# The first layer's shift computed with its weights stationary, as columns

## The reference, cut to what matters

```python
def _modulation(cond, w_mod, b_mod):
    m = jax.nn.silu(cond) @ w_mod + b_mod
    return jnp.split(m, 3, axis=-1)
...
sh, sc, g = _modulation(c, w_mod[l], b_mod[l])
shc, scc, gc = _modulation(c_ctx, w_mod[l], b_mod[l])
h = x * (1.0 + sc) + sh
hc = ctx * (1.0 + scc) + shc
q, k, v, z = jnp.split(h @ w_in[l], 4, axis=-1)
...
```

## Time and profile before

| | us |
|---|---|
| median of 3 runs | 1850.63 |
| lowest, highest run | 1850.36, 1851.28 |
| the profiled execution | 1850.39 |
| its span | 1848.6 |
| TensorE busy | 1802.8 (98% of the span) |
| VectorE busy | 1291.5 (70%) |
| ScalarE busy | 928.0 (50%) |
| GpSimd busy | 269.4 (15%) |

### The profile page before, as it was taken

The page is one execution under the profiler, slowest core; times in us unless marked ns, Lnnn a source line. Parts: engine busy times, 40 slices in busy tenths (PEclk is TensorE's granted clock), DMA queues, the critical chain, the costliest instruction groups (busy, mean ns, idle before and its releaser), DMA issues. The chain is left out here.

```text
span 1848.6 us, 30835 instructions
## 1 busy us (share of the span) xinstructions
PE 1802.8 (98%) x10621; PEld 1554.1 (84%) x10621; DVE 1291.5 (70%) x2061; ACT 928.0 (50%) x1680; POOL 269.4 (15%) x219
## 2 busy tenths in 40 slices
PE   7999999999999999989999999999999999999998
PEld 3888888888888888878878889888888888898886
DVE  6677777778687877765868485675848484757658
ACT  2555555555555555560046555464736464554500
POOL 3100000000000000255431010101000010102951
PEclk9999999999999999999999999999999999999999
DMA  9512121312122222225420010101010100101343
GB/s 348 135 47 83 47 82 47 84 38 79 54 74 60 74 60 62 73 94 187 159 80 24 12 45 11 45 0 45 11 45 11 34 23 11 45 11 45 99 143 125
DMA packets 82111, 127.28 MB, mean 69 GB/s; under 512 B 49760, under 2 KB 49920, under 8 KB 81936
## 3 DMA queue, kind: packets, MB, share of 16 engines
q1 hardware_dynamic: 76048, 108.54, 18.7%
q0 software_dynamic: 2384, 8.39, 1.6%
q10 hardware_dynamic: 3632, 9.73, 1.3%
HBM read 108.90 MB, written 20.09 MB: 70 GB/s over the span
## 5 line engine op out<-in xcount | busy, mean ns | idle before, releaser
L548 PE MATMUL acc<-h_hi,w_hi 128*128 128x512 f32 (+1 forms) x1408 | 524.9, 373 | 3.1 <-DVE h_lo L473 1.6
L548 PE MATMUL acc<-h_hi,w_lo 128*128 128x512 f32 (+1 forms) x1408 | 508.7, 361 | 0.0
L548 PE MATMUL acc<-h_lo,w_hi 128*128 128x512 f32 (+1 forms) x1408 | 507.9, 361 | 0.0
L548 PEld LDWEIGHTS acc<-h_hi,w_lo 128*128 128x128 f32 x1408 | 265.3, 188 | 41.5
L548 PEld LDWEIGHTS acc<-h_hi,w_hi 128*128 128x128 f32 x1408 | 265.8, 189 | 40.3 <-DVE h_lo L473 4.7
L548 PEld LDWEIGHTS acc<-h_lo,w_hi 128*128 128x128 f32 x1408 | 266.3, 189 | 33.9
L1676 DVE TENSOR_REDUCE stats<-acc 128x1 f32<-128x1280 f32 x128 | 189.7, 1487 | 43.3 <-PE acc L1775 42.7
L1586 ACT ACTIVATE far_prob<-acc,stats 128x1280 f32<-128x1280 f32 x128 | 170.2, 1330 | 28.3 <-DVE stats L1676 26.5
L1593 ACT ACTIVATE far_pt<-acc 128x512 f32<-128x512 f32 (+1 forms) x192 | 101.1, 527 | 162.0 <-PE acc L1784 158.6
L1775 PE MATMUL acc<-k_dup,q_stack 128*128 128x512 f32 (+1 forms) x768 | 176.7, 367 | 1.8 <-ACT far_prob L1586 0.4
L1797 PE MATMUL acc<-far_pt,far_v 128*128 128x128 f32 x1280 | 172.7, 275 | 0.0
(11 more groups left out here) (208 smaller groups left out, 2906.8 us busy)
## 6 DMA issues: line engine op xcount, KB each, us to landing
w_raw<-in_w_in SPq DMA_DIRECT2D x64, 512.0 KB, 3.3
near_late_slots<-in_w_mod SPq DMA_DIRECT2D x64, 256.0 KB, 2.7
w_raw<-in_w_out SPq DMA_DIRECT2D x16, 512.0 KB, 3.2
w_raw<-y_t POOLq DMA_DIRECT2D x14, 448.0 KB, 5.0
y_t<-y SPq DMA_DIRECT2D x7, 640.0 KB, 3.1
modulation_rows<-in_w_scale SPq DMA_DIRECT2D x8, 512.0 KB, 6.9
modulation_rows<-in_w_mod SPq DMA_DIRECT2D x8, 512.0 KB, 6.7
out_rows<-in_x SPq DMA_DIRECT2D x8, 512.0 KB, 4.5
```

The lines of the kernel that those rows point to most:

```text
L548: mm = nc.tensor.matmul(m.bank(self.bank_of(j, c), w), wt[:, b % 2, k, :], ht[:, k, t0:t0 + w], start=(k == 0 and i == 0), stop=(k == KT - ...
```

## The change

The operands of the shift's products change places. Each piece of weights is now stationary, in eight blocks of 128x128, and the two condition columns move (128x2). Each product is 128x2: both conditions' shift of 128 channels, as columns. The 64 products (8 pieces by 8 blocks) are not added in PSUM; each has its own two columns of bank 3 (`shift_parts`, 128 columns in all). When all are there VectorE adds the eight pieces' with one reduction, then scales by 0.5 and adds the bias with a second operation. `take_rows` on ScalarE and `turn_rows` on TensorE are gone. `cols_done` now goes up to 3. Since only bank 3 is held, TensorE transposes the tokens of n = 0, 1 and 2 ahead of the wait, which stands before n = 3.

```diff
-        self.row_buf = m.k_raw[0:2, 0:D]
+        self.shift_parts = m.psum[:, 3, 0:2 * KT * KT]
...
-    def take_rows(self, act):
-        act.wait_ge(self.piece_used, KT)
-        for half in range(2):
-            self.nc.scalar.activation(self.row_buf[:, half * 512:(half + 1) * 512], self.m.psum[0:2, 2 + half, :], ACT.Copy,
-                                      scale=0.5).then_inc(self.row_ready, 1)
...
-        v.wait_ge(self.turned, 1)
-        first = m.b_cols[:, 0, 0:1]
-        nc.vector.tensor_tensor(m.mod_cols[:, 0, :, 0:KT], m.bank(2, 2 * KT).rearrange("p (k c) -> p c k", c=2),
-                                bass.AP(first.tensor, first.offset, [list(first.ap[0]), [0, 2], [1, KT]]), ALU.add)\
+        v.wait_ge(self.piece_used, KT)
+        shift, first = m.mod_cols[:, 0, :, 0:KT], m.b_cols[:, 0, 0:1]
+        nc.vector.tensor_reduce(shift, self.shift_parts.rearrange("p (k t c) -> p c t k", k=KT, c=2), AX, ALU.add)\
+            .then_inc(self.cols_done, 1)
+        v.wait_ge(self.cols_done, 2)
+        nc.vector.scalar_tensor_tensor(shift, shift, 0.5,
+                                bass.AP(first.tensor, first.offset, [list(first.ap[0]), [0, 2], [1, KT]]), ALU.mult, ALU.add)\
             .then_inc(self.cols_done, 1)
...
-            for half in range(2):
-                mm = nc.tensor.matmul(m.psum[0:2, 2 + half, :], m.cond_act[:, :, k], self.pieces[k][:, half * 512:(half + 1) * 512],
-                                      start=(k == 0), stop=(k == KT - 1))
+            for t in range(KT):
+                mm = nc.tensor.matmul(self.shift_parts[:, 2 * (k * KT + t):2 * (k * KT + t + 1)],
+                                      self.pieces[k][:, t * P:(t + 1) * P], m.cond_act[:, :, k], start=True, stop=True)
             mm.then_inc(self.piece_used, 1)
-
-    def turn_rows(self, pe):
-        pe.wait_ge(self.row_ready, 2)
-        for k in range(KT):
-            mm = self.nc.tensor.transpose(self.m.psum[:, 2, 2 * k:2 * k + 2], self.row_buf[:, k * P:(k + 1) * P], self.m.ident[0:2, 0:2])
-        mm.then_inc(self.turned, 1)
...
-                modulation.take_rows(act)
-                act.wait_ge(modulation.cols_done, 2)
+                act.wait_ge(modulation.cols_done, 3)
...
-                    if n == 2:
-                        modulation.turn_rows(pe)
-                        pe.wait_ge(modulation.cols_done, 2)
+                    if n == 3:
+                        pe.wait_ge(modulation.cols_done, 3)
```

More of the change, by code:

```diff
@@ L208, in __init__ @@
         self.tanh_done, self.cond_ready, self.coef_ready, self.piece_used = sem("tanh"), sem("cond"), sem("coef"), sem("used")
-        self.row_ready, self.turned, self.scale_done, self.cols_done = sem("row"), sem("turned"), sem("scale"), sem("cols")
+        self.scale_done, self.cols_done = sem("scale"), sem("cols")
         self.dve, self.lam_exp = sem("dve"), sem("lam_exp")
-        self.row_buf = m.k_raw[0:2, 0:D]
+        self.shift_parts = m.psum[:, 3, 0:2 * KT * KT]
         self.unused = [b[:, 0:D] for b in (m.gate, m.y)]
```

## The result

| | before | changed |
|---|---|---|
| median, us (12 runs each) | 1850.36 | 1854.64 |
| lowest and highest, us | 1850.04, 1851.30 | 1854.00, 1856.39 |
| profiled execution, us (its span) | 1850.39 (1848.6) | 1854.89 (1853.0) |
| its mean granted clock of TensorE | 0.999 | 0.991 |

The changed kernel takes 1.0024 times the time of before, 95% interval 1.0016 to 1.0031: slower by 4.28 us. The forecast was 0.65 us faster. What happened is rival B, a clock of 1.2 GHz under the narrow products.

The account below looks back on a forecast made before the run. TensorE, busy 98%, bounds the kernel; its start waits for loads. Modulation 1.28 us earlier, cut by token landings to 0.94, then 0.65, takes the 1850.63 median to 1849.98, so 1850.0; range 1849.2 to 1856.6.

Parts of the forecast that it names:

- rival B: TensorE's clock falls to 1.2 GHz under the shift's narrow products: +4.3 to +6.8 us, likeliest +5.5, 1856.1; chance 0.32.
- the paragraph on the clock: TensorE's shift products: clock taken to stay at 1.00, as it did from 31.9 to 36.9 us in the kernel before.
- the price of a piece: TensorE's 16 passes on each piece of the shift's weights: 1.84 us, against 1.88 before.
- columns ready: VectorE's reduction and bias operation with hand-overs finish the shift's columns 0.53 us after the last product, at 32.37 us.
- uncovered tokens: Token transposes on TensorE cannot start before their transfer lands at 32.73 us, whatever the shift does.
- the fifth tile's wait: TensorE waits for the first tokens' second half, landing at 35.4 us, before the fifth tile's transposes.
- the first projection: First projection matmul on TensorE starts at about 35.95 us instead of 36.89, 0.94 us earlier.
- the pause's end: TensorE's pause for VectorE's low part of the second weights ends at 59.07 us instead of 59.72.
- The wait at the ninth tile: TensorE waits half a microsecond for the second token group, landing at 40.8 us; the gain becomes 0.65 us.
- the gain reaches the end whole: After 60 us TensorE never waits for a transfer, so the 0.65 us should reach the kernel's end.
- the slow time after it: After the late first projection, work runs slow until the clock is back: up to 1.8 us lost.
- Rival C: Token loads land early, without the gate at 40.8 us: the whole 1.28 us comes through, 1849.35; chance 0.04.

Follow-up runs that it names:

- e1: The changed kernel with 64 moving columns instead of 2 in each of the shift's matmuls; 1854.04 us, ratio 1.0018.
- e5: e1 with 128 moving columns instead of 64; 1850.58 us against 1850.70 for the kernel before, ratio 0.9998.
- e7: The changed kernel with 16 transposes of 128 columns per piece in place of the shift's 8 matmuls; 1850.50 us, ratio 1.0001.
- e2: The changed kernel with one matmul of 512 moving columns ahead of the wait for each piece but the first; 1863.94 us, ratio 1.0078.
- e4: e1 with the fifth tile's projection done before the ninth tile's transposes; 1854.36 us, ratio 1.0019.
- e3: The changed kernel with four 128x128 transposes ahead of the wait for each piece but the first; 1858.04 us, ratio 1.0041.
- e6: e5 with the fifth tile's projection done before the ninth tile's transposes; 1850.24 us, ratio 0.9998.
- e8: The kernel before with the second half of each piece but the first left out of the products; 1853.22 us in one run.

## Why the prediction was wrong

**The step that failed** is the paragraph on the clock. It asked the right question and chose the wrong row. The row that I went by, a clock of 1.00 from 31.9 to 36.9, was in the main a stretch of transposes with 128 moving columns each, twenty of them; only eight passes, 0.65 us, were narrow. I read it as a sign that thin work holds the clock, and counted weight loads, which fill TensorE as much as before, as work. e1, e5 and e7 against the changed kernel show that neither follows: loads of stationary tiles with 2 moving columns leave TensorE 100% busy in the profile and at 1.2 GHz. So the term that failed is the price of a piece: 1.84 us in the forecast's sum, 16 x 0.211 = 3.38 us once the clock had fallen at 14.9 us. With it the last product came at 37.94 and not at 31.84. The number that should have weighed more stood in rival B's own argument: 2048 moving columns per piece before, 32 after.

The measured 1854.64 lies inside the stated range of 1849.2 to 1856.6. It does so because the range took in the nearer half of B, not because the forecast's mechanism came near it.

**The chain's own terms** were right. A piece at the high level costs 1.84 us (first 16 passes of e2's run: 1.85); the reduction 0.28 (0.29); columns ready 0.53 us behind the last product (0.54); uncovered tokens at 32.73 (32.90 in e5), the fifth tile's wait, the first projection, and the pause's end, each within 0.2 us in e5. The wait at the ninth tile was over-sized: forecast 0.5 us, measured 0.2. That the gain reaches the end whole is shown for one run only: in e5's profile 0.8 us are left at TensorE's last matmul, and the medians differ by 0.12.

**Rival B's terms.** 3.4 us a piece (16 x 0.211 = 3.38) and last product at 37.2 (37.94, as the clock fell at 14.9 and not at 16.8). First projection at 41.6 (41.97). Mis-sized was the slow time after it, up to 1.8 us: the clock rose at 42.2, 0.2 us into the first projection, so under 0.1 us of that was paid (41.97 to 42.38 for the first matmul, 36.89 to 37.22 before). B's likeliest price of 5.5 us came out as 4.28 (1854.64, forecast for B 1856.1); the low end of its range, 4.3, was the value. The spread of the runs, 2.4 us against 1.3 for the kernel before, goes with the clock: its mean is 0.990 in the slowest run (1856.39), 0.991 in the three next and 0.992 or 0.993 in those under 1854.4. So the time at the low level varies from run to run; whether it is the fall that comes at varying times (16.7 and 17.7 us in e4 and e1, whose products are alike), the one profile of the changed kernel can't show.

**Sums that don't add up**, none of which moves the forecast. A piece has four passes of 512 columns in the kernel before, not sixteen. Rival C's 1.28 us could not have come through, since the fifth tile's wait already cuts the gain to 0.94. In B, 37.2 and 4.2 make 41.4 and not 41.6, and 4.7 and 1.8 make +6.5 and not +6.8.

**The rule on transposes.** The Trainium skill, "TensorE: Matmul & The Clock Gate", Part 4: PE-mode transpose, says that transposes don't count as work the way matmuls do, and that the clock isn't raised for them. Carried over to matmuls of two columns it gave rival B's time: the right outcome for a wrong reason. e7 contradicts the rule as it stands: 19 us of transposes held 1.00. In e3 and e4 the clock rose from 0.50 with nothing but transposes before it for 4 and 3 us. The stretch at 1.2 GHz was one of weight loads with next to nothing moving behind them, which the rule doesn't mention.

**Beating both kernels.** e5 and e6 remove what makes the change slow. By their medians neither is measurably faster than the kernel before; half of their runs have a shorter span than any of its runs on that chip, by 0.2 to 0.7 us. The stage waits for the tokens' transfers as soon as the shift is out of the way: the first projection came 0.88 us earlier in e5, and there is hardly more in it.

## What to carry to other kernels

Swapping the operands so that the large one was stationary and two columns moved raised TensorE's busy time between 12 and 38 us from 19.5 to 26.0 us, and halved its clock there. Before such a swap, ask what will still move through the array and not only whether TensorE stays busy, and afterwards read the granted clock of the stretch; what TensorE does next pays as well. If the swap is wanted for its output's shape, moving the few columns repeated up to the width of the weight load cost little here (2.06 us instead of 1.84 for a piece, hidden behind the arrivals) and held the clock.

## What the runs showed that I had not expected

- A busy share of 100% beside a granted clock of 0.50 for 27 us. Busy time in the profile does not tell the clock.
- Transposes held the clock as matmuls of the same width did (e7, e5), and it rose under them alone (at 47.0 us in e3 and at 40.6 in e4, both ahead of the first projection).
- 64 moving columns per pass, in bursts with waits between, let the clock fall at 17.7 us; 128 held it (e1, e5).
- Taking work away from TensorE made the kernel before slower, by 2.9 us in one run, 1.75 of them in this stage (e8).
- The clock can fall once more far from the change: at 795 us in e8 and at 802 us in e2, and not in the eight other profiles. Only the delay at several places of the timeline tells the two apart.
